# Bringing x into the odd mixer through memory blocks, with merged last down groups and a later exponential of the forget gate

## The chip, the cores and the metric

The kernel runs on one core of one Trainium2 chip. The metric is the device time of one execution in microseconds (us), as the median of the runs shown. The instruction streams are called by their engines: TensorE (PE in the profile), VectorE (DVE), ScalarE (ACT), GpSimd (POOL) and SyncE (SP). SP only issues transfers here, and ACT and POOL issue some of theirs.

## The reference

A block of 256 tokens with 2048 features goes through two layers, all in float32:

```python
def reference(x, ...):
    for i in range(2):
        h = rms_norm(x, norm_mix_g[i])
        if i % 2 == 0:      # even mixer: spatial gating and pooling
            ...
        else:               # odd mixer: attention with a forget gate, 16 heads of 128
            p = h @ w_in_odd[o]
            q, k, v = ...                         # columns 0:2048, 2048:4096, 4096:6144
            f_logit = p[..., 3 * C_WIDTH:] + b_forget[o]      # 16 columns
            log_f = jax.nn.log_sigmoid(f_logit)
            att = forgetting_attention(q, k, v, log_f)
            mix = att @ w_out_odd[o]
        x = x + mix
        x = x + conv_ffn(rms_norm(x, norm_ffn_g[i]), w_up[i], conv_w[i], conv_b[i], w_down[i])
    return rms_norm(x, final_norm_g)
```

`conv_ffn` multiplies with `w_up` (2048 x 11264), convolves over three tokens, gates with a silu and multiplies with `w_down` (5632 x 2048). In `forgetting_attention` the running sum `c` of `log_f` over the tokens is added to the logits of each head: `logits + c[q] - c[k]`, ahead of the softmax.

## The kernel before

**Weights.** All weights stream through the core once, in pieces of 1 MB (128 x 2048 numbers), 368 of them in a fixed order. SP loads piece c into slot c % 4 of `raw`. ACT rounds it to TensorE's single-pass format (`high`, L466, into `w_high`), DVE takes the rest (`low`, L878, into `w_low`), and TensorE multiplies with both. Each activation is split in the same way, into `h_split` or `y_split`, so a product is three passes: high by high, high by low and low by high. ACT and DVE work three pieces ahead of TensorE (`LEAD = 3`): in step c they prepare piece c + 3, which waits until TensorE has used piece c - 1. `load(c + 4)` waits until DVE is done with piece c. The order of the instructions on each engine is written out by hand; semaphores tie the engines together, and `fenced` makes an engine wait for its own instruction.

**The end of layer 0.** The feed-forward part takes `w_up` in 11 groups (`NG`) of features. For each of them a down product of four pieces adds to the 256 x 2048 block `x`: a piece covers 512 features of the group and 512 columns of `x`. The four blocks of 512 columns are called column 0 to column 3 here, and the eight last down pieces D0 to D7: before, D0 to D3 are group 9 on columns 0 to 3, and D4 to D7 group 10 on columns 0 to 3. DVE adds each product to `x` from PSUM (`add_to_x`, L940).

**From x to the mixer.** The odd mixer needs `x` with the features on the partitions. Columns 0, 1 and 2 are turned by TensorE (`transpose_x`, L1511, called from `down` with `transposes=True`, eight 128 x 128 transposes a column into PSUM), column 3 by 16 transposes of DVE in 32 x 32 blocks (`turn_blocks`, L931). Then ACT scales with the norm's gain and rounds (`turned_high`, L505), and DVE takes the rest (`turned_low`, L899); `s_turned` counts the columns that are ready (9 to 12 here). The squares of `x` are summed on ACT (`squares`, L488), and the norm's factor per token is spread over the rows by DVE (`spread_rstd`, L970).

**The first mixer pieces**, called M0 to M11, in this order: M0, M1 = v parts 0, 1; M2, M3 = first halves of the panels q0, k0; M4, M5 = v parts 2, 3; M6, M7 = second halves of q0, k0; M8 to M11 = q1 and k1. v part n needs column n, and a half panel two columns. After M3 TensorE computes the forget gate's sums (`forget_sums`, L1783); ACT copies them (L760), DVE adds up and scales, ACT takes an exponential and a logarithm (L763, L764, each behind a load of its function table), and DVE runs the sum over the tokens (L1323), whose end (`cneg`, L1327) raises `s_cq`. On that wait POOL, which stores the 16 rows to memory (L422), loads them spread over all partitions (L432, L434) and adds the causal mask (L437, `s_bias`), and TensorE's first scores.

**The heads.** From M8 on each head goes: scores on TensorE (`scores`), logits with bias and row maximum on DVE (`head_logits`, L1259), exponentials on ACT, one reciprocal on DVE, scaling on ACT, 16 small transposes on DVE (`head_blocks`, L1281), then the product with v on TensorE (`attend`, L1773), a rounding on ACT and the rest on DVE (`head_low`, L1287). Here `attend` waits for both `head_blocks` and the `head_low` of the head before. These steps stand between the weight pieces on each engine:

```python
if k == 10:
    head_blocks(hh, r)
...
if h is not None:
    head_logits(h, psA[:, 2, :], r)      # first group: h = 0 in step 9, h = 1 in step 11
...
low(c + k + LEAD, r)
```

Of the kernel before, what the change touches and what calls it, by code (L numbers as in the profile page):

```python
# [29 lines left out]
P = 128  # L30
RING = 4
LEAD = 3
# [17 lines left out]
def build(nc, x_in, norm_mix_g, norm_ffn_g, final_norm_g, w_in_even, ln_v_g, ln_v_b, w_spatial,  # L50
          b_spatial, w_pool, pool_scale, w_out_even, w_in_odd, b_forget, w_out_odd, w_up, conv_w,
          conv_b, w_down, out, c_dram):
# [21 lines left out]
    N_END = N_FFN[1] + 12 * NG  # L74
    OUT0_ORDER = [(c, q) for c in range(4) for q in (2, 3, 0, 1)]
# [8 lines left out]
    A_OUT0, A_FFN, A_OUT1 = 0, [4, 4 + 4 * NG + 4], 4 + 4 * NG  # L84
# [6 lines left out]
    X_READY = [0, A_OUT0, A_FFN[0] + 4 * (NG - 1), A_OUT1, A_FFN[1] + 4 * (NG - 1)]  # L91
# [8 lines left out]
    OUT = out[0].rearrange("(t p) d -> p t d", p=P)  # L100

    with ExitStack() as ctx:
# [67 lines left out]
        xT = [work[:, c0:c0 + 1024].rearrange("p (k t) -> p k t", k=4) for c0 in (0, 1024, 2048, 4096)]  # L170
        scaled = raw[:, 0:2, :]
# [34 lines left out]
        s_turn = sem("x_turned")  # L206
        s_turn_hi = sem("turned_high")
# [75 lines left out]
        def turned_bank(s, n, kk):  # L283


            if s == 0 and n == 0:
                return psT[:, min(kk, 2), TOK * (kk // 3):TOK * (kk // 3) + TOK]
            if s in (1, 3) or (s, n) in ((0, 3), (2, 3)):
                return xT[n if s else 0][:, kk, :]
            return psT[:, 2 * (n % 2) + kk // 2, TOK * (kk % 2):TOK * (kk % 2) + TOK]  # L290
# [9 lines left out]
        def _(sp):  # L300
# [47 lines left out]
            def load_ffn(l):  # L348
# [24 lines left out]
                down(B + 124, NG - 2)  # L373
                down(B + 128, NG - 1)
# [71 lines left out]
        def _(a):  # L446
# [47 lines left out]
            def turned_high(s, n):  # L494
# [3 lines left out]
                for kk in range(4):  # L498
# [150 lines left out]
            def ffn(l):  # L649
# [40 lines left out]
                for k in range(16):  # L690
                    if k >= 14 and l == 0:
                        turned_high(s + 1, k - 14)
# [30 lines left out]
                    if l == 0 and k >= 13:  # L723
                        squares(s + 1, k - 13)
# [131 lines left out]
        def _(ve):  # L856
# [64 lines left out]
            def turn_blocks(s, n, tokens):  # L921
# [10 lines left out]
                if 3 in tokens:  # L932
                    ins.then_inc(s_turn, 1)

# [233 lines left out]
            def ffn(l):  # L1168
# [48 lines left out]
                for k in range(16):  # L1217
                    if k >= 14 and l == 0:
                        turned_low(s + 1, k - 14)
                    low(c + k + LEAD)  # L1220
                    if k == 0:
# [18 lines left out]
                    if k >= 8 and not (l == 1 and k >= 12):  # L1240
# [50 lines left out]
            def heads_of_group(first, r=0):  # L1291
                c, hh = N_MIX1 + 12 * first, 4 * first
                for k in range(12):
                    if first == 0 and k == 0:
                        turned_low(2, 2)
                        turn_blocks(2, 3, (0, 1))
                        mean_square(2)
                        turn_blocks(2, 3, (2, 3))
                    if first == 0 and k == 1:
                        rstd_columns(2)  # L1300
                    if first == 0 and k == 2:
                        turned_low(2, 3)
# [9 lines left out]
                    if first == 0 and k == 5:  # L1312
# [8 lines left out]
                        link(ve.tensor_scalar(fl, fl, 0.0, None, ALU.min))  # L1321
                        ve.wait_ge(s_fe, 1)
# [5 lines left out]
                    low(c + k + LEAD, r)  # L1328
                    if h is not None:
                        head_inverse(h, r)  # L1330
                    if first == 0 and k == 2:
                        spread_rstd()
                        link(ve.tensor_scalar(q_rstdT, rstdT[:, :], float(P) ** -0.5, None, ALU.mult))
# [531 lines left out]
```

## Time and profile before

| | |
|---|---|
| median of 3 runs | 2085.55 us (2085.26 to 2085.55) |
| profiled execution | 2085.45 us, span of its instructions 2083.8 us |
| granted TensorE clock, mean | 0.999 |
| busy: TensorE, DVE, ACT, POOL | 2075.3, 1595.5, 1053.6, 26.0 us |
| moved | 397.17 MB, mean 191 GB/s |

The span runs from the first to the last instruction; 1.65 us of the execution's time lie around it. TensorE's ends are modelled, so its groups in a timeline overlap the next one's start by a few tenths; the distance between two starts is the safer measure.

### The profile page before, as it was taken

Reading aid. Unit: us, or ns where it says so; the run is one execution under the profiler, and the core shown is the slowest. Engines: PE = TensorE matmul, PEld = TensorE weight load, DVE = VectorE, ACT = ScalarE, POOL = GpSimd, SP = SyncE. Lnnn points to the kernel's source line nnn. Section 1 sums busy time; section 2 is a strip of 40 time slices with the busy share of each in tenths; the row PEclk is TensorE's granted clock in tenths of the full one; section 3 lists DMA queues with packets and bytes.
Section 4 is the critical chain, followed back from the end, with each engine's and each line's share of the span. In section 5 each row is a group of like instructions: output and inputs, shape, how many; then the busy total and the mean of one; then the engine's idle time right before and its main releaser. Section 6 shows DMA issues by size and latency. Waiting matters only on the chain.

```text
span 2083.8 us, 29774 instructions
## 1 busy us (share of the span) xinstructions
PE 2075.3 (100%) x10936; PEld 1793.1 (86%) x10936; DVE 1595.5 (77%) x2058; ACT 1053.6 (51%) x1103; POOL 26.0 (1%) x56
## 2 busy tenths in 40 slices
PE   9999999999999999999999999999999999999998
PEld 8888888888888888888888888888888888888887
DVE  7988886777667776778788788997776677767676
ACT  7554564445444544456544454465454445444454
POOL 0000000000000000000100000000000000000000
PEclk9999999999999999999999999999999999999999
DMA  8656565655565655655565565556555556556553
GB/s 281 221 164 220 179 206 181 201 195 184 184 198 183 203 181 181 201 187 169 185 214 157 189 209 183 169 187 216 193 185 187 195 183 205 182 181 200 182 191 113
DMA packets 317636, 397.17 MB, mean 191 GB/s; under 512 B 8676, under 2 KB 241420, under 8 KB 317452
## 3 DMA queue, kind: packets, MB, share of 16 engines
q1 hardware_dynamic: 313948, 391.40, 56.7%
q0 software_dynamic: 1056, 3.16, 0.7%
q10 hardware_dynamic: 2576, 1.85, 0.3%
q8 instruction: 36, 0.59, 0.1%
q14 instruction: 20, 0.16, 0.0%
HBM read 394.28 MB, written 2.11 MB: 190 GB/s over the span
## 4 chain that ended last, share of the span: by engine, by line
PE 100%; DVE 0%; issue 0%; ACT 0%; DVEq 0%; ACTq 0%
PE ps_turned L1443 38%; PE ps_straight L1482 35%; PE ps_turned L1452 20%; PE ps_straight L1443 1%; PE ps_turned L1482 1%; PE ps_straight L1452 1%; PE ps_straight L1530 1%; PE ps_straight L1763 0%; PE ps_straight L1773 0%; PE ps_turned L1511 0%; PE ps_straight L1518 0%; PE ps_straight L1638 0%; PE ps_straight L1783 0%; PE ps_straight L1710 0%; PE ps_straight L1707 0%; PE ps_straight L1706 0%
## 5 line engine op out<-in xcount | busy, mean ns | idle before, releaser
L878 DVE TENSOR_TENSOR w_low<-w_raw,w_high 128x2048 fp32r<-128x2048 f32 x368 | 842.3, 2292 | 327.2 <-ACT w_high L466 296.9
L466 ACT ACTIVATE w_high<-w_raw 128x2048 fp32r<-128x2048 f32 x367 | 702.6, 1918 | 659.2 <-PE ps_straight L1482 280.6
L1443 PE MATMUL ps_turned<-h_split,w_high 128*128 128x512 f32 x3456 | 802.9, 390 | 0.0
L1443 PEld LDWEIGHTS ps_turned<-h_split,w_high 128*128 128x128 f32 x3456 | 643.7, 188 | 130.4
L1452 PEld LDWEIGHTS ps_turned<-h_split,w_low 128*128 128x128 f32 x3456 | 425.4, 192 | 6.2 <-DVE w_low L878 0.2
L1452 PE MATMUL ps_turned<-h_split,w_low 128*128 128x256 f32 x3456 | 429.2, 283 | 0.0
L1482 PE MATMUL ps_straight<-w_high,y_split 128*128 128x512 f32 x1792 | 425.5, 390 | 0.1
L1482 PEld LDWEIGHTS ps_straight<-w_high,y_split 128*128 128x128 f32 x1792 | 336.0, 188 | 70.0 <-issue 0.5
L1482 PE MATMUL ps_straight<-w_low,y_split 128*128 128x512 f32 x896 | 221.3, 389 | 0.0
L1482 PEld LDWEIGHTS ps_straight<-w_low,y_split 128*128 128x128 f32 x896 | 168.2, 188 | 34.9
L1149 DVE SCALAR_TENSOR_TENSOR work<-work,conv_columns 128x256 f32<-128x256 f32 x352 | 154.6, 481 | 11.0
L940 DVE TENSOR_TENSOR x<-x,ps_straight 128x512 f32<-128x512 f32 x182 | 116.8, 683 | 54.3 <-PE ps_straight L1482 53.5
L632 ACT ACTIVATE work<-work,conv_columns 128x256 f32<-128x256 f32 x176 | 95.6, 591 | 60.1 <-DVE work L888 60.0
L475 ACT ACTIVATE work<-ps_turned 128x512 f32<-128x512 f32 x108 | 64.7, 599 | 79.7 <-PE ps_turned L1443 66.0
L884 DVE TENSOR_TENSOR work<-ps_turned,work 128x512 f32<-128x512 f32 x108 | 74.5, 690 | 27.6 <-ACT work L475 24.8
L1482 PE MATMUL ps_straight<-w_high,h_split 128*128 128x512 f32 x352 | 85.6, 395 | 0.0
L1281 DVE STREAM_TRANSPOSE work<-work 32x96 f32<-32x96 f32 x256 | 69.1, 270 | 13.1 <-DVE small L1269 7.9
L1482 PEld LDWEIGHTS ps_straight<-w_high,h_split 128*128 128x128 f32 x352 | 65.5, 188 | 13.3
L888 DVE TENSOR_TENSOR work<-work,rstd_rows 128x512 f32<-128x512 f32 x103 | 71.3, 692 | 3.5
L931 DVE STREAM_TRANSPOSE work<-x 32x256 f32<-32x256 f32 x160 | 69.8, 436 | 2.4
L1482 PE MATMUL ps_straight<-w_low,h_split 128*128 128x512 f32 x176 | 43.6, 389 | 0.0
L1482 PEld LDWEIGHTS ps_straight<-w_low,h_split 128*128 128x128 f32 x176 | 33.0, 188 | 6.9
(210 smaller groups left out, 777.7 us busy)
## 6 DMA issues: line engine op xcount, KB each, us to landing
w_raw<-in_w_up SPq DMA_DIRECT2D x176, 1024.0 KB, 5.0
w_raw<-in_w_down SPq DMA_DIRECT2D x88, 1024.0 KB, 5.0
w_raw<-in_w_in_odd SPq DMA_DIRECT2D x48, 1024.0 KB, 5.4
w_raw<-in_w_in_even SPq DMA_DIRECT2D x22, 1024.0 KB, 5.7
w_raw<-in_w_out_even SPq DMA_DIRECT2D x16, 1024.0 KB, 5.0
w_raw<-in_w_out_odd SPq DMA_DIRECT2D x16, 1024.0 KB, 5.1
w_raw<-in_w_in_even SPq DMA_DIRECT2D x4, 512.0 KB, 5.9
work<-c_rows POOLq DMA_DIRECT2D x8, 256.0 KB, 6.4
```

The source lines that it names most:

```text
L466: a.activation(wh[:, s, :], raw[:, s, :], ACT.Copy).then_inc(s_high, 1)
L632: ins = a.activation(cc[j % 2][:, m, :], up[:, m, 2:], ACT.Identity, scale=taps[:, l, 2, bass.ds(i, 1)], bias=taps[:, l, 3, bass.ds(i, 1)])
L878: ve.tensor_tensor(wl[:, s, :], raw[:, s, :], wh[:, s, :].bitcast(F32), ALU.subtract).then_inc(s_low, 1)
L884: fenced(ve.tensor_tensor(to, src, spare, ALU.add), s_added, at(q + 1, 4, r))
L888: return ve.tensor_tensor(ap, ap, factor.unsqueeze(1).to_broadcast([P, 2, TOK]), ALU.mult)
L931: ins = ve.transpose(dst, src)
L940: ins = ve.tensor_tensor(xc, xc, psA[:, 2 * (i % 2) + t, :] if sums is None else sums[:, t, :], ALU.add)
L1149: ins = ve.scalar_tensor_tensor(out=c[:, m, :], in0=up[:, m, 2 - back:TOK + 2 - back], scalar=taps[:, l, 2 - back, bass.ds(i, 1)], in1=c[: ...
L1281: ins = ve.transpose(dst, src)
L1443: ins = pe.matmul(ps[:, 2 * slot + m, :], hi[:, kk, P * m:P * m + P], acts[:, K, :], start=(K == 0 and not narrow_ran), stop=(K == KC - 1) ...
L1452: ins = pe.matmul(ps[:, 2 * slot + m, TOK:], lo[:, kk, P * m:P * m + P], acts[:, K, 0:TOK], start=(K == 0 and opens), stop=(K == KC - 1), ...
L1482: return pe.matmul(ps[:, 2 * slot + t, :], acts[:, k0 + kk, a0:a0 + P], weights[:, kk, :], start=begin, stop=end)
```

## The change

The down pieces of the last two groups of layer 0 are taken in another order (`LAST0`, as (second group, column)): both groups of a column add up in PSUM, and `add_to_x` runs once per column: column 0 after D3, column 1 after D4, column 2 after D5, column 3 after D7. As soon as a column is summed, ACT issues four stores of it to a buffer in device memory (`x_dram`, 128 KB each). When they have landed, SP issues four loads that bring it back with the 32 x 32 blocks already in their turned places, in runs of 32 numbers (128 bytes; `X_BLOCKS`). One transpose of DVE then turns all blocks of the column (128 x 1024). TensorE's transposes of `x` for the odd mixer and DVE's 16 block transposes of column 3 go away. The loads stand in SP's queue between those of the mixer pieces, two columns behind the load of M3, one behind M4's, one behind M5's. The forget gate's sums move from ahead of M4 to ahead of M5, ACT's copies of them from step 5 to step 6, and the exponential and logarithm from ahead of step 5's rounding to the end of step 6, behind the rounding of M9 and `copy_low_half`. DVE's scan moves likewise.

```diff
+    LAST0 = [(0, 0), (0, 1), (0, 2), (1, 0), (1, 1), (1, 2), (0, 3), (1, 3)]
+    X_COLUMNS = x_dram.rearrange("n a t i c -> n i a t c")
+    X_BLOCKS = x_dram.rearrange("n a t i (k j b) -> n j a (t i k) b", k=4, j=4)
...
+        blocks = [work[:, c0:c0 + 1024] for c0 in (0, 1024)]
@@ SP
+            def fetch_blocks(n):
+                sp.wait_ge(s_column[n], 64)
+                if n >= 2:
+                    sp.wait_ge(s_turn, 4 * 2 + n - 1)
+                for j in range(4):
+                    sp.dma_start(blocks[n % 2][32 * j:32 * j + 32, :].rearrange("p (m b) -> p m b", b=32),
+                                 X_BLOCKS[n, j]).then_inc(s_blocks[n % 2], 16)
             for n, (j, k) in enumerate(MIX1_FIRST):
                 load(N_MIX1 + n, quad(W_IN1, k, 8) if j == "v" else half(W_IN1, k, 256 * (j // 2) + D * (j % 2)))
+                if n == 3:
+                    fetch_blocks(0)
+                    fetch_blocks(1)
+                if n in (4, 5):
+                    fetch_blocks(n - 2)
@@ ACT
+            def store_column(n):
+                a.wait_ge(s_xadd, X_READY[2] + n + 1)
+                for i in range(4):
+                    a.dma_start(X_COLUMNS[n, i], x[32 * i:32 * i + 32, :, 512 * n:512 * n + 512])\
+                        .then_inc(s_column[n], 16)
...
-                    if k >= 14 and l == 0:
-                        turned_high(s + 1, k - 14)
+                    if k == 15 and l == 0:
+                        turned_high(2, 0)
                     high(c + k + LEAD)
-                    if l == 0 and k >= 13:
-                        squares(s + 1, k - 13)
+                    if l == 0 and 12 <= k < 15:
+                        store_column(k - 12)
+                        squares(2, k - 12)
@@ ACT, heads_of_group
                     if first == 0 and k == 0:
-                        turned_high(2, 2)
+                        turned_high(2, 1)
+                        store_column(3)
                         squares(2, 3)
                     if first == 0 and k == 2:
+                        turned_high(2, 2)
+                    if first == 0 and k == 3:
                         turned_high(2, 3)
-                    if first == 0 and k == 5:
+                    if first == 0 and k == 6:
                         a.wait_ge(s_f, 1)
                         a.activation(f_xl, psA[0:HEADS, 2, TOK:], ACT.Copy).then_inc(s_fT, 1)
                         fenced(a.activation(f_wl, psA[2 * HEADS:3 * HEADS, 2, 0:TOK], ACT.Copy), s_fT, 2)
-                        a.wait_ge(s_fl, 1)
-                        link(a.activation(fe, fe, ACT.Exp))
-                        fenced(a.activation(fe, fe, ACT.Ln, bias=1.0), s_fe, 1)
                     high(c + k + LEAD, r)
                     if k in ((5, 7, 9, 11) if first else (6, 7, 9, 11)):
                         copy_low_half(Q_MIX1 + 4 * first + j, j % 2, c + k, r)
+                    if first == 0 and k == 6:
+                        a.wait_ge(s_fl, 1)
+                        link(a.activation(fe, fe, ACT.Exp))
+                        fenced(a.activation(fe, fe, ACT.Ln, bias=1.0), s_fe, 1)
@@ DVE
+            def turn_within_blocks(n):
+                ve.wait_ge(s_blocks[n % 2], 64 * (n // 2 + 1))
+                ve.transpose(xT[2 + n % 2].rearrange("p k (g a) -> p k g a", a=32),
+                             blocks[n % 2].rearrange("p (g k b) -> p k g b", g=8, k=4)).then_inc(s_turn, 1)
...
-                    if k >= 14 and l == 0:
-                        turned_low(s + 1, k - 14)
+                    if k == 15 and l == 0:
+                        turn_within_blocks(0)
+                        turned_low(2, 0)
                     low(c + k + LEAD)
+                    if k == 15 and l == 0:
+                        turn_within_blocks(1)
+                        add_to_x(X_READY[2] + 3, 3, c + k)
+                        turned_low(2, 1)
-                    if k >= 8 and not (l == 1 and k >= 12):
+                    if l == 0 and k in (11, 12, 13):
+                        add_to_x(X_READY[2] + k - 11, k - 11, c + k, sums=psT if k == 13 else None)
@@ DVE, heads_of_group: turn_within_blocks(2) and turned_low(2, 2) ahead of low in step 2; turn_within_blocks(3),
@@ turned_low(2, 3) and spread_rstd behind it; the scan behind take_qk(0) in step 6
@@ TensorE
-                    if transposes and n >= 1:
-                        transpose_x(2, n - 1)
+            def last_two_down0(c):
+                pe.wait_ge(s_actlo, 2 * NG - 2)
+                for n, (second, q) in enumerate(LAST0):
+                    ...
+                    straight_quad(c + n, (0, 1, 0, 1)[q], Y, 4 * second, second == 0, second == 1,
+                                  ps=psT if q == 2 else psA)
@@ TensorE, heads_of_group
-                        pe.wait_ge(s_turned, 9 + min(k, 2) if k < 4 else 12)
+                        pe.wait_ge(s_turned, (9, 10, 10, 10, 11, 12)[min(k, 5)])
-                        if k == 4:
+                        if k == 5:
                             forget_sums()
```

## Rows read from the trace of the kernel before

**Rows 1.** The page: shares by engine in the chain that ended last.

```profile
PE 100%; DVE 0%; issue 0%; ACT 0%; DVEq 0%; ACTq 0%
```

**Rows 2.** Waits of TensorE over the whole span: in total, times, longest.

```profile
PE ps_straight L1518 <- DVE ones L862: 1.2, 1, 1.2
```

**Rows 3.** Timeline of TensorE, D5 to M0: start, length, engine, line, tiles, count.

```profile
951.77 3.79 PE L1482 MATMUL ps_straight<-w_high,y_split 128*128 128x512 f32 x16
...
957.21 1.03 PE L1511 MATMUL ps_turned<-ident,x 128*128 128x128 f32 x8
...
970.68 3.89 PE L1482 MATMUL ps_straight<-w_high,h_split 128*128 128x512 f32 x16
```

**Rows 4.** Timeline of DVE, 915 to 1030: as before, idle time ahead in brackets.

```profile
957.41 1.28 DVE L940 TENSOR_TENSOR x<-x,ps_straight 128x512 f32<-128x512 f32 x2 [1.09 <-PE ps_straight L1482]
...
962.09 2.29 DVE L878 TENSOR_TENSOR w_low<-w_raw,w_high 128x2048 fp32r<-128x2048 f32 x1 [1.13 <-issue]
...
965.63 1.68 DVE L899 SCALAR_TENSOR_TENSOR h_split<-ps_turned,feature_columns,h_split 128x256 fp32r<-128x256 f32 x4
...
990.61 3.98 DVE L970 STREAM_TRANSPOSE rstd_rows<-small 32x64 f32<-32x64 f32 x16
...
1005.11 0.68 DVE L1323 TENSOR_TENSOR_SCAN work<-work 16x256 f32<-16x256 f32 x1 [3.30 <-ACT work L764]
...
1006.82 0.28 DVE L1327 TENSOR_SCALAR work<-work 16x256 f32<-16x256 f32 x1
...
1024.88 0.74 DVE L1259 SCALAR_TENSOR_TENSOR work<-ps_straight,small,work 128x128 f32<-128x128 f32 x2 [1.21 <-PE ps_straight L1763]
```

**Rows 5.** DMA, whole span: SP's queue, then issues with KB and us to landing.

```profile
q1 hardware_dynamic: 313948, 391.40, 56.7%
...
w_raw<-in_w_down SPq DMA_DIRECT2D x88, 1024.0 KB, 5.0
...
result<-w_raw SPq DMA_DIRECT2D x3, 128.0 KB, 1.9
```

**Rows 6.** DMA in 890 to 900 us: the queue of ACT's own transfers.

```profile
q10 hardware_dynamic: 2096, 0.13, 14.1%
```

**Rows 7.** A stretch: length, busy times by engine, clock, DMA share, GB/s.

```profile
12.00:16.00 4.00, 4.00 (x21) 3.32 (x20) 2.78 (x2) 0.89 (x1) 0.00 (x0) 1.00 1.05 389
```

**Rows 8.** Timeline of ACT, 885 to 1030.

```profile
958.34 1.71 ACT L505 ACTIVATE h_split<-ps_turned,feature_columns 128x256 fp32r<-128x256 f32 x4 [3.03 <-PE ps_turned L1511]
960.09 1.92 ACT L466 ACTIVATE w_high<-w_raw 128x2048 fp32r<-128x2048 f32 x1
...
1001.57 1.28 ACT L763 ACT_TABLE_LOAD   x1 [4.14 <-DVE work L1319]
...
1004.59 0.42 ACT L764 ACTIVATE work<-work 16x256 f32<-16x256 f32 x1
...
1013.12 0.60 ACT L475 ACTIVATE work<-ps_turned 128x512 f32<-128x512 f32 x1 [3.59 <-PE ps_turned L1443]
```

**Rows 9.** Groups of DVE by shape: busy, mean ns of one.

```profile
L931 DVE STREAM_TRANSPOSE work<-x 32x256 f32<-32x256 f32 x160 | 69.8, 436 | 2.4
L1281 DVE STREAM_TRANSPOSE work<-work 32x96 f32<-32x96 f32 x256 | 69.1, 270 | 13.1 <-DVE small L1269 7.9 <-DVE work L888 1.9
```

**Rows 10.** Timeline of POOL, 1000 to 1060: the bias of heads 0, 1, then 2, 3.

```profile
1007.76 0.66 POOL L422 DMA_DIRECT2D c_rows<-work  x1 [1005.07 <-DVE work L1327]
...
1017.17 2.17 POOL L437 TENSOR_TENSOR work<-work,causal 128x256 f32<-128x256 f32 x2 [5.80 <-DMA work<-c_rows]
...
1047.64 1.43 POOL L437 TENSOR_TENSOR work<-work,causal 128x256 f32<-128x256 f32 x2 [5.35 <-DMA work<-c_rows]
```

**Rows 11.** Timeline of DVE, 1059 to 1130: the rest of head 2.

```profile
1076.89 0.42 DVE L1287 TENSOR_TENSOR y_split<-ps_straight,y_split 128x256 f32 x1 [0.18 <-DVE work L1281]
```

**Rows 12.** Timeline of TensorE, 1022 to 1110: products with v of heads 0 and 3.

```profile
1042.01 0.59 PE L1773 MATMUL ps_straight<-work 128*128 128x256 f32 x2
...
1078.32 0.59 PE L1773 MATMUL ps_straight<-work 128*128 128x256 f32 x2
```

More of the change, by code:

```diff
@@ L51, in build @@
           b_spatial, w_pool, pool_scale, w_out_even, w_in_odd, b_forget, w_out_odd, w_up, conv_w,
-          conv_b, w_down, out, c_dram):
+          conv_b, w_down, out, c_dram, x_dram):
     D = x_in.shape[2]
@@ L206, in build @@
         s_turn = sem("x_turned")
+        s_column = [sem(f"x_column_stored{i}") for i in range(4)]
+        s_blocks = [sem(f"x_blocks_landed{i}") for i in range(2)]
         s_turn_hi = sem("turned_high")
@@ L372, in load_ffn @@
                 panels(B + 120, NG - 1, 1)
-                down(B + 124, NG - 2)
-                down(B + 128, NG - 1)
+                if l == 0:
+                    for n, (second, q) in enumerate(LAST0):
+                        row = 4 * (NG - 2 + second)
+                        load(B + 124 + n, W_DOWN[l][:, row:row + 4, 512 * q:512 * q + 512])
+                else:
+                    down(B + 124, NG - 2)
+                    down(B + 128, NG - 1)
             load_ffn(0)
@@ L1321, in heads_of_group @@
                         link(ve.tensor_scalar(fl, fl, 0.0, None, ALU.min))
+                    low(c + k + LEAD, r)
+                    if h is not None:
+                        head_inverse(h, r)
+                    if first == 0 and k == 2:
+                        turn_within_blocks(3)
+                        turned_low(2, 3)
+                        spread_rstd()
+                        link(ve.tensor_scalar(q_rstdT, rstdT[:, :], float(P) ** -0.5, None, ALU.mult))
+                    if k in ((5, 7, 9, 11) if first else (6, 7, 9, 11)):
+                        take_qk((k - 5) // 2, first, r)
+                    if first == 0 and k == 6:
                         ve.wait_ge(s_fe, 1)
@@ L1327, in heads_of_group @@
                         fenced(ve.tensor_scalar(cneg, sums[0:HEADS, :], -1.0, None, ALU.mult), s_cq, 1)
[L1328 to L1333, printed above, removed]
-                    if k in ((5, 7, 9, 11) if first else (6, 7, 9, 11)):
-                        take_qk((k - 5) // 2, first, r)
             heads_of_group(0)
@@ L1679, in panel, with down @@
                 turned_panel(c, j, H, r)
-            def down(l, g, c, r=0, frm=0, transposes=False):
-                if frm:
-                    pe.wait_ge(s_actlo, 22 * l + 2 * g + 2)
-                else:
-                    pe.wait_ge(s_actlo, at(22 * l + 2 * g + 2, 2, r))
+            def down(l, g, c, r=0):
+                pe.wait_ge(s_actlo, at(22 * l + 2 * g + 2, 2, r))
                 for n in range(4):
@@ L1689, in down @@
                     pe.wait_ge(s_xadd, at(i - 1, 4, r))
[L1690 to L1692 removed]
+                    straight_quad(c + n, n % 2, Y, 0, True, True, r)
+            def last_two_down0(c):
+                pe.wait_ge(s_actlo, 2 * NG - 2)
+                for n, (second, q) in enumerate(LAST0):
+                    if n == 0:
+                        pe.wait_ge(s_xadd, X_READY[2] - 1)
+                    if n == 1:
+                        pe.wait_ge(s_xadd, X_READY[2])
+                    if n == 2:
+                        pe.wait_ge(s_added, Q_FFN[0] + 4 * NG - 1)
+                    if n == 3:
+                        pe.wait_ge(s_actlo, 2 * NG)
+                    if n == 6:
+                        pe.wait_ge(s_xadd, X_READY[2] + 2)
+                    straight_quad(c + n, (0, 1, 0, 1)[q], Y, 4 * second, second == 0, second == 1,
+                                  ps=psT if q == 2 else psA)
             def last_down(c):
@@ L1742, in ffn @@
                     panel(l, NG - 1, j, B + 116 + 2 * j)
-                down(l, NG - 2, B + 124)
                 if l == 0:
-                    down(l, NG - 1, B + 128, frm=1, transposes=True)
+                    last_two_down0(B + 124)
                 else:
+                    down(l, NG - 2, B + 124)
                     last_down(B + 128)
```

21 lines of the change are left out of this document (11 added, 10 removed).

## The prediction

> **What bounds the kernel now.** I read the chain of waits first: TensorE alone makes up the chain that ended last [rows 1]. The list of waits says the same from the other side: TensorE's longest wait on another engine is 1.2 us, once, at the start [rows 2]. So a step on ACT, DVE, POOL or a queue costs nothing as long as TensorE finds its operand ready, and the change can win only what it takes from TensorE's own instructions. What it can lose is every place where an operand comes later than TensorE wants it. The rest is therefore a comparison of arrival times around the end of layer 0 and the first heads. The sum goes against the profiled execution, 2085.45 us (2083.8 us of span and 1.65 around it), 0.1 us under the median of the runs.
>
> **What TensorE saves.** D5 starts at 951.77 and the first transposes at 957.21, so a straight piece takes 5.44 us [rows 3]. From 951.77 to M0 at 970.68 stand three pieces and three sets of transposes: 18.91 us, against 3 x 5.44 = 16.32 without the transposes. The saving is 2.59 us, and M0 could start at 957.21 + 2 x 5.44 = 968.09, M1 at 973.53. The new order of the down pieces has the same eight pieces, so it costs TensorE nothing. The four additions to x that go are DVE's, 1.28 us each [rows 4]; DVE is off the chain, so I count them at nothing.
>
> **Columns through memory.** Column 0 is summed after D3, which ends at 951.77 - 5.44 = 946.3; with the addition of 1.28 us [rows 4] it is there at 947.8, columns 1 and 2 at 953.2 and 958.7. ACT issues four stores; one of 128 KB landed 1.9 us after its issue [rows 5], so with four issues in a row and weights beside them I take 4 us: 952. SP then issues the loads, but behind M3's weights, which go out when DVE is done with D7's low half (950.9) and take 5.0 us [rows 5]: the blocks start at 956. A column is 4096 runs of 128 bytes, 256 on each of 16 engines. No row shows 128-byte runs. The nearest are the forget gate's weights, 2048 runs of 64 bytes: 2096 packets took 14.1% of 10 us x 16 engines, 10.8 ns each [rows 6]. From above I bound them by the mean of SP's packets, 56.7% x 2083.8 x 16 / 313948 = 60 ns [rows 5], though those carry ten times the bytes. I take 12 ns: 3.1 us a column; column 0 lands at 959 to 960. In the upper bound it is 15.4 us.
>
> The Trainium skill has a rule against such runs: "DMA: Bandwidth & Descriptors", Specifications, asks for 512 B at least for line rate and says that shorter runs are read, modified and written. Read as a quarter of the full rate of 389 GB/s [rows 7], that is an estimate of 5.4 us a column instead of 3.1; column 0 would land near 962, and the sum below would change by under 1 us. The 64-byte packets at 10.8 ns [rows 6] stand at 5.9 GB/s an engine, so the loss of rate is real here and its size is open.
>
> DVE comes to the first transpose after the low half of M1: ACT rounds that piece after D5 (957.4 + 1.92 [rows 8]), DVE takes 2.29 us more [rows 4]: 961.8. The blocks have then been there for about 2 us. The transpose of 128 x 1024 has no row; a line through 270 ns at 96 elements and 436 at 256 [rows 9] gives 1.04 ns an element and 1.24 us. The column then needs 1.71 us on ACT, and DVE's 1.68 us that start behind ACT's first half [rows 8, 4]: column 0 is ready at 965.9, 2.2 us before M0. Next on ACT M2's rounding (1.92), on DVE its low half (2.29), the transpose of column 1 (1.24), column 3's addition (1.28), then the split of column 1: 965 + 1.9 + 2.3 + 1.3 + 1.3 + 1.7 with the hand-overs (about 0.1 each) is 973.9. M1 wants it at 973.5, so TensorE waits 0.4 us. Columns 2 and 3 follow in the same way, each behind a rounding and a low half, column 3 also behind its own store and load: I get 988 against M4 at 990.5, and 995.7 against the gate's sums at 996. No wait, with 0.3 us to spare on the second. SP's weights behind the loads lose some 3 to 9 us, and no TensorE piece wants them for more than 10. The DVE step spread_rstd (3.98 us [rows 4]) now stands behind column 3, which makes M6 and M7 later on DVE (1002, 1004.5) but not late (1005, 1010.7). **After M6** TensorE is 2.59 - 0.4 = 2.2 us ahead.
>
> **The forget gate's running sum.** This edit I do not cost at nothing. The exponential now waits for `copy_low_half`, which waits for the end of M6. Before, that copy started at 1013.12 [rows 8]; with TensorE 2.2 us ahead it starts at 1010.9 and ends at 1011.5. The two table loads and two functions take 1004.59 + 0.42 - 1001.57 = 3.44 us [rows 8]: 1015.0. DVE from the scan to the end of `cneg` takes 1007.10 - 1005.11 = 2.0 us [rows 4]: `s_cq` at 1017.1, where it was 1007.1, that is 10.0 us later. Behind it stands POOL: from `cneg` to a bias that is ready it took 1017.17 + 2.17 - 1007.10 = 12.2 us; with the next tile's addition of 1.43 it is 11.5 [rows 10]. I take 11.5, since DVE stands idle beside it now: bias at 1028.6. Before, it was ready at 1019.3, and DVE used it at 1024.88 [rows 4] when the scores came; the cover was 5.5 us, and the delay is 9.3. So the first head's logits come 3.7 us later than before, in absolute time. Behind them in DVE's order wait the low half of M12 and all that follows, TensorE not yet. About 0.7 us comes back, because ACT's next copy no longer waits for TensorE; the chain of heads runs 3.0 us late.
>
> Its cover is short. The rest of head 2 ended at 1076.89 + 0.42 = 1077.3 [rows 11], and TensorE asked for it at 1078.32 [rows 12]: 1.0 us of slack. The heads follow one another on DVE and ACT with hardly any idle time, so a delay is handed down from head to head. By head 3 TensorE is where that chain is, less the slack: 3.0 - 1.0 = 2.0 us later than before. It had been 2.2 ahead, so the waits at the products with v add up to 4.2 us. In the next group DVE waits for TensorE again, and nothing more is lost or won back.
>
> **Sum.** 2085.45 - 2.59 + 0.4 + 4.2 = 2087.4 us, 0.1% above before. What a measurement of this kernel can tell from no change is 0.2%, or 4.2 us.
>
> **Rivals.**
> *The saving is kept.* Bias ready by 1025 instead of 1028.6 would leave the heads on time; then the time is 2085.45 - 2.59 plus the 0 to 0.4 us at M1: 2082.9 to 2083.3. For it speaks only that POOL's 11.5 us rest mostly on transfers that were shared with weights; against it that the second tile's transfers took as long. Anything between this and the forecast is a shorter bias wait.
> *Both waits grow.* If the runs cost 25 to 40 ns, column 0 lands at 962 to 966 and what follows shifts: 1 to 4 us at M1, handed on to M6, to the exponential and to the heads in full, and more at column 1 above 30 ns. The time is 2089 to 2095.
> *Slower, by the loads.* At the upper bound of 60 ns a column takes 15.4 us on SP's queue, with the next column and M4's weights behind it. Column 0 lands at 971 (TensorE waits 7 us at M0), column 1 at 986.5 (10 at M1), column 2 after M4's weights at 1004.5 (1 at M4), column 3 at 1022.6 (13 at the gate's sums); with the 4 us of the heads 2085.45 - 2.6 + 31 + 4 = 2118. It decides from about 30 ns a run. The rows speak against it, since 64 bytes cost 10.8 ns [rows 6], but runs that are read from memory only just written have no row. The Trainium skill's "DMA: Bandwidth & Descriptors", Rules for kernel authors, warns more sharply: a plain DMA with a rearranged access pattern took 19 times as long as a hardware transpose. That would be an estimate of 19 x 1.35 = 26 us a column (512 KB at 389 GB/s [rows 7] being 1.35) and beyond 2150; the runs here keep 128 bytes in order, and no run here shows such a price.
> *Faster by more than 4.2 us* has no source, since TensorE has no idle time to give back.
>
> **How the numbers follow.** The forecast (2085 to 2089.6) has 0.63, the saving kept or mostly kept 0.13, both waits grown 0.11, the loads 0.10, something unseen on the fast side 0.03. The predicted time is the first one's, 2087.4. The range 2083.2 to 2091 leaves out the loads, the upper half of the grown waits, the fast end and a little of the kept saving, 0.2 in all. Within 0.2% are the first two, 0.76; slower 0.21; faster 0.03.
>
> **What would show it.** In the profile after: no transposes between D5 and M0, and 5.44 us between starts; the loads of a column landing 3 to 4 us after M3's weights; a first wait of TensorE at M1 under 1 us; the scan near 1015 instead of 1005; POOL's first addition near 1027; DVE idle ahead of the first logits (L1259 in the numbering before) for some 5 us; and waits of TensorE of 1 to 2 us at the products with v of heads 0 to 3. The prediction is wrong if the first column lands after 962, if those products do not wait, or if TensorE waits at M4 or at the gate's sums.

## The result and the profile after

The changed kernel took 2089.14 us in the median of 20 runs (2088.10 to 2090.75), the kernel before 2085.43 (2084.95 to 2085.60): a ratio of 1.0018, with an interval of 1.0012 to 1.0024. That is 3.7 us more, 1.7 above the forecast and inside its range. The interval does not reach 1, so a change of this size, 0.18%, can be told from none, although the prediction put that limit at 0.2%. The profiled execution took 2089.85 us, with a span of 2088.1.

TensorE's waits on other engines in the changed kernel, over the whole span (in total, times, longest), answer to [rows 2]. Line 1827 is the first matmul of `scores`, 1838 that of the product with v, 927 the scaling of a panel (`take_qk`), 1333 `head_blocks`:

```profile
PE ps_straight L1827 <- DVE work L927: 2.9, 1, 2.9
PE ps_straight L1571 <- DVE ones L901: 1.2, 1, 1.2
PE ps_straight L1838 <- DVE work L1333: 0.6, 1, 0.6
PE ps_straight L1583 <- DVE w_high L954: 0.3, 1, 0.3
```

Two are new. The timeline of TensorE shows the stretch of [rows 3], from D6 to M1:

```profile
956.71 3.79 PE L1535 MATMUL ps_straight<-w_high,y_split 128*128 128x512 f32 x16
...
962.14 3.79 PE L1535 MATMUL ps_straight<-w_high,y_split 128*128 128x512 f32 x16
...
967.59 3.79 PE L1535 MATMUL ps_straight<-w_high,h_split 128*128 128x512 f32 x16
...
973.23 3.92 PE L1535 MATMUL ps_straight<-w_high,h_split 128*128 128x512 f32 x16
```

The steps are 5.43 and 5.45 us, and M1 starts 5.64 after M0: a wait of 0.2 us. The gate's sums start at 995.53, 5.63 after M4: again some 0.2 us of wait. TensorE then asks for the first scores at 1021.36, where it did so at 1024.03 before: it is 2.7 us ahead, 0.5 of them because D5 already starts that much earlier. So 2.2 of the 2.59 us are still there, and what the change loses beyond that comes behind. Further on in the same timeline, which answers to [rows 12]:

```profile
1021.36 0.38 PE L1827 MATMUL ps_straight<-work 128*128 128x128 f32 x2
...
1040.08 0.70 PE L1838 MATMUL ps_straight<-work 128*128 128x256 f32 x2 [0.58 <-DVE work L1333]
...
1049.35 0.80 PE L1827 MATMUL ps_straight<-work 128*128 128x128 f32 x2 [2.86 <-DVE work L927]
1049.94 1.06 PE L1828 MATMUL ps_straight<-work 128*128 128x256 f32 x2
1050.44 6.40 PE L1535 MATMUL ps_straight<-w_high,h_split 128*128 128x512 f32 x16
...
1058.50 0.59 PE L1838 MATMUL ps_straight<-work 128*128 128x256 f32 x2
...
1082.55 0.59 PE L1838 MATMUL ps_straight<-work 128*128 128x256 f32 x2
```

and in the kernel before the first scores, the scores of head 2 and the product behind them:

```profile
1024.03 0.38 PE L1762 MATMUL ps_straight<-work 128*128 128x128 f32 x2
...
1048.14 0.38 PE L1762 MATMUL ps_straight<-work 128*128 128x128 f32 x2
...
1054.27 0.59 PE L1773 MATMUL ps_straight<-work 128*128 128x256 f32 x2
```

The product of head 3 starts 4.2 us after its place before. TensorE waits 0.6 us at the first product and 2.9 at the scores of head 2, and then M13's 16 matmuls take 6.40 us where M12's took 3.92. From 1049.35 to 1058.50 it needs 9.15 us; before, the same work took 1054.27 - 1048.14 = 6.13. The 3.0 us are no wait. Stretches of the changed kernel (length, busy times of TensorE, weight loads, DVE, ACT, POOL, then the granted clock, DMA share, GB/s) say what they are:

```profile
1044.00:1046.40 2.40, 2.40 (x12) 1.72 (x10) 2.26 (x2) 0.93 (x5) 1.13 (x2) 1.00 0.92 312
1046.40:1049.30 2.90, 0.09 (x1) 0.00 (x0) 1.38 (x2) 2.38 (x5) 0.00 (x0) 0.90 0.99 247
1049.30:1050.40 1.10, 1.05 (x4) 0.96 (x5) 0.77 (x3) 1.10 (x1) 0.00 (x0) 0.50 0.84 261
1050.40:1052.00 1.60, 1.60 (x5) 1.31 (x4) 1.52 (x7) 1.60 (x2) 1.26 (x2) 0.50 1.00 356
1052.00:1054.00 2.00, 2.00 (x6) 1.53 (x5) 1.91 (x8) 0.36 (x1) 0.16 (x1) 0.50 0.16 57
1054.00:1056.00 2.00, 2.00 (x7) 1.52 (x7) 1.58 (x3) 0.00 (x0) 0.00 (x0) 0.62 0.00 0
1056.00:1058.00 2.00, 2.00 (x10) 1.68 (x9) 1.97 (x4) 0.00 (x0) 0.00 (x0) 1.00 0.00 0
```

The granted clock falls to 0.50, the lower of its two levels (1.2 of 2.4 GHz), in the wait, and is back at 1.00 after some 6 us of work at half speed: 1.10, 1.60, 2.00 and, by the mean of 0.62, 0.76 of the next 2.00, together 6.2 us. Half speed loses half of that, 3.1 us, which accounts for the 3.0.

Why the scores wait is read from DVE's timeline of the changed kernel, which answers to [rows 4]:

```profile
1014.61 0.68 DVE L1384 TENSOR_TENSOR_SCAN work<-work 16x256 f32<-16x256 f32 x1 [1.99 <-ACT work L824]
...
1016.32 0.28 DVE L1388 TENSOR_SCALAR work<-work 16x256 f32<-16x256 f32 x1
...
1028.43 0.74 DVE L1311 SCALAR_TENSOR_TENSOR work<-ps_straight,small,work 128x128 f32<-128x128 f32 x2 [5.84 <-POOL work L464]
...
1047.88 0.69 DVE L923 TENSOR_TENSOR work<-ps_turned,work 128x512 f32<-128x512 f32 x1 [1.63 <-ACT work L502]
1048.61 0.69 DVE L927 TENSOR_TENSOR work<-work,rstd_rows 128x512 f32<-128x512 f32 x1
```

and POOL's, which answers to [rows 10]:

```profile
1017.27 0.66 POOL L449 DMA_DIRECT2D c_rows<-work  x1 [1014.58 <-DVE work L1388]
...
1026.90 1.43 POOL L464 TENSOR_TENSOR work<-work,causal 128x256 f32<-128x256 f32 x2 [6.04 <-DMA work<-c_rows]
```

The running sum is ready at 1016.6 instead of 1007.1, the bias 11.7 us behind it, at 1028.3, and DVE stands idle for 5.84 us ahead of the first logits. Behind them in its order stand the logits of head 1 and then panel k1 (`take_qk(3)`), ready at 1049.3: that is what the scores of head 2 wait for. In the kernel before the panel's last step was

```profile
1045.76 0.69 DVE L888 TENSOR_TENSOR work<-work,rstd_rows 128x512 f32<-128x512 f32 x1
```

so it was ready at 1046.45, 1.7 us ahead of the scores at 1048.14. Now it comes 2.9 us later and TensorE 1.7 earlier, at 1046.5; less the 1.7 of slack, that is the wait.

### The profile page after: what moved, and what is told of

The parts are those of the page before. It is cut to its first block, busy times and chain, and to the rows that moved or that the text cites. A ratio compares the mean times of both kernels' runs of the same rounds, so it can differ in the third digit from the quotient of the medians.

```text
span 2088.1 us, 29692 instructions
## 1 busy us (share of the span) xinstructions
PE 2076.0 (99%) x10912; PEld 1792.0 (86%) x10912; DVE 1588.0 (76%) x2038; ACT 1053.6 (50%) x1103; POOL 25.2 (1%) x56
## 4 chain that ended last, share of the span: by engine, by line
PE 92%; DVE 5%; issue 1%; ACT 1%; POOL 0%; DMA 0%; DVEq 0%; ACTq 0%; POOLq 0%
PE ps_turned L1496 35%; PE ps_straight L1535 32%; PE ps_turned L1505 19%; DVE w_low L917 2%; DVE work L970 1%; PE ps_turned L1535 1%; PE ps_straight L1496 1%; PE ps_straight L1583 1%; DVE work L1194 0%; PE ps_straight L1505 0%; DVE x L985 0%; DVE h_split L938 0%; PE ps_straight L1828 0%; DVE work L927 0%; DVE work L923 0%
## 5 line engine op out<-in xcount | busy, mean ns | idle before, releaser
L1535 PE MATMUL ps_straight<-w_high,y_split 128*128 128x512 f32 x1760 | 417.7, 390 | 0.1
L1535 PEld LDWEIGHTS ps_straight<-w_high,y_split 128*128 128x128 f32 x1760 | 330.1, 188 | 68.9 <-issue 0.6
L985 DVE TENSOR_TENSOR x<-x,ps_straight 128x512 f32<-128x512 f32 x172 | 110.3, 682 | 52.5 <-PE ps_straight L1535 51.8
L970 DVE STREAM_TRANSPOSE work<-x 32x256 f32<-32x256 f32 x144 | 62.8, 436 | 2.2
L532 ACT ACTIVATE h_split<-work,feature_columns 128x256 fp32r<-128x256 f32 x52 | 23.7, 504 | 41.5 <-DVE work L970 29.6
```

Source lines behind the costliest of these rows:

```text
L970: ins = ve.transpose(dst, src)
L985: ins = ve.tensor_tensor(xc, xc, psA[:, 2 * (i % 2) + t, :] if sums is None else sums[:, t, :], ALU.add)
L1535: return pe.matmul(ps[:, 2 * slot + t, :], acts[:, k0 + kk, a0:a0 + P], weights[:, kk, :], start=begin, stop=end)
```

## The experiments

Theory A: the late exponential makes the bias late, with it DVE's chain of the first heads, and TensorE waits for that chain and then runs at the low clock. Theory B: the columns' way through memory costs the time. Times are medians of 10 or 11 runs, beside the kernel before in the same set (2085.4 to 2085.6). The changed kernel took 2089.14 in its first set and 2089.20 in a later one.

**One part undone.** On ACT and likewise on DVE, against the changed kernel:

```diff
@@ ACT, step 6, behind the copies of the gate's sums
+                        a.wait_ge(s_fl, 1)
+                        link(a.activation(fe, fe, ACT.Exp))
+                        fenced(a.activation(fe, fe, ACT.Ln, bias=1.0), s_fe, 1)
@@ DVE: the scan from the end of step 6 to step 5, ahead of low
```

> The changed kernel with only the order of the forget gate undone: exponential and logarithm stand on ACT right behind the copies of the gate's sums again, ahead of the rounding of M9, and DVE's scan stands ahead of the low half of M8. Theory A (the late running sum costs the time: bias late, DVE's heads late, TensorE waits at the second head pair's scores and then runs at the low clock): the scan ends near 1012 instead of 1016.6, the bias is ready near 1023 instead of 1028.3, TensorE waits neither at the first product with v (0.6 us in the changed kernel) nor at the scores of head 2 (2.9), and the clock stays at 1.0. DVE is now held by the scan and may bring the addition of panel q0 1 to 1.5 us late for M8. Time 2083.0 to 2084.6. Rival B (the columns' way through memory costs the time, in bandwidth or in late weights): no change against the changed kernel, 2088 to 2090.

Measured: 2085.39 us, ratio 0.9999 (0.9990 to 1.0008); 3.7 less than the changed kernel, 0.8 above the expected range. No wait at the products or the scores, and the clock is 1.0. The bias was ready only at 1026.3, not near 1023, and TensorE still did not wait for what hangs on it. The new wait is at M8. The trace names no releaser for it; in the kernel M8 waits for DVE's addition of panel q0, which ended at 1018.31. A second wait of 0.5 us stands at the gate's sums. TensorE's timeline of this run, M8:

```profile
1018.40 3.91 PE L1494 MATMUL ps_turned<-h_split,w_high 128*128 128x512 f32 x16 [1.50 <-issue]
```

So the later exponential bought something too: the early one holds DVE 3.7 us at the scan, with the panel behind it. The two waits give back most of what the transposes saved.

**One part alone.** The kernel before, with only the exponential, the logarithm and the scan moved as the change moves them.

> The kernel before with only the exponential, the logarithm and the scan put behind the rounding and the copy of step 6, as the change does; the columns still go through TensorE. Theory A: the scan waits for the end of M6 as in the changed kernel, which here is 2.6 us later; sum ready near 1019.3, bias near 1031, the first logits 6 us later than before; TensorE waits about 0.7 us at the first product with v and 3 us at the scores of head 2, and loses 3 us more at the low clock behind that wait: 2091 to 2093. Rival B: the later exponential is hidden, 2085.2 to 2086.

Measured: 2090.86 us, ratio 1.0026 (1.0017 to 1.0036), 0.1 under the expected range. This edit alone costs 5.3 us, and theory B has nothing to work with here, since no column goes through memory. TensorE's waits in this run have the same places as in the changed kernel:

```profile
PE ps_straight L1764 <- DVE work L889: 2.9, 1, 2.9
PE ps_straight L1520 <- DVE ones L863: 1.2, 1, 1.2
PE ps_straight L1775 <- DVE work L1282: 0.4, 1, 0.4
```

and M13 behind them is as slow as there, at a clock of 0.50 from 1052 to 1058:

```profile
1053.07 6.39 PE L1484 MATMUL ps_straight<-w_high,h_split 128*128 128x512 f32 x16
```

**The wait filled.** The changed kernel, in the first group of heads only:

```diff
+                    if fill and k == 0:
+                        pe.wait_ge(s_added, Q_MIX1 + 3)
+                        for _ in range(10):
+                            pe.matmul(psT[:, 0, :], H[:, 0, 0:P], H[:, 0, :], start=True, stop=True)
                     if first and k in (0, 2):
                         scores(hh - 2 + k // 2, SB, first - 1, r)
```

> The changed kernel with ten matmuls that no one reads (128 x 512 into a free PSUM bank, some 2.2 us) in TensorE's wait ahead of the scores of head 2, in the first group of heads alone. Clock theory: the wait lasts as long as before (until DVE is done with panel k1), but TensorE is not idle in it, the granted clock stays at 1.0 and the scores and M13 take 0.5 and 5.7 us again instead of 1.1 and 8.1: 3 us less than the changed kernel, 2085.7 to 2086.5. Rival (M13 is slow for another reason, such as the transfers or DVE beside it): the same as the changed kernel, 2088.5 to 2090.

Measured: profiled 2087.97 us, median 2088.48 (1.0014, 1.0005 to 1.0023). The clock is 1.00 in every stretch from 1040 to 1058, and M13's matmuls take 3.99 us. TensorE's timeline:

```profile
1046.60 2.43 PE L1884 MATMUL ps_turned<-h_split 128*128 128x512 f32 x10
1049.74 0.46 PE L1827 MATMUL ps_straight<-work 128*128 128x128 f32 x2 [0.71 <-DVE work L927]
1050.04 0.60 PE L1828 MATMUL ps_straight<-work 128*128 128x256 f32 x2
1050.28 3.99 PE L1535 MATMUL ps_straight<-w_high,h_split 128*128 128x512 f32 x16
...
1080.55 0.67 PE L1838 MATMUL ps_straight<-work 128*128 128x256 f32 x2 [0.41 <-issue]
```

The profile confirms the mechanism: what made M13 slow is the clock behind an idle TensorE. The gain is smaller than expected: the median is 2.0 us above the clock theory's range and at the lower end of the rival's. The product of head 3 comes 2.2 us after its place before, and it waits there: with the clock held, TensorE runs into DVE's chain again (the trace names no releaser; the rest of head 2 on DVE ended 0.1 us ahead of it). The median fell by only 0.7 us, and that against another set, so I ran the changed kernel again beside one with 16 filling matmuls.

> The changed kernel with 16 unread matmuls (3.5 us) instead of 10 ahead of the scores of head 2, so that TensorE is not idle there in any repetition; where the wait is the 2.9 us of the trace they make it 0.6 us longer. Clock theory: M13 and the scores run at full speed (3.0 us less), 0.6 us are given back, so 2.4 us less than the changed kernel in the same set: 2086.5 to 2087.2. If the low clock plays a smaller part in the repeated runs than in the profiled one, as the medians of the run with ten matmuls suggested (0.7 us less instead of 1.9), it is 2088 to 2089.5.

> The changed kernel once more, unaltered, beside the run above on the same chip: 2088.8 to 2089.5, with waits at the first product with v and at the scores of head 2 as in its first profile.

Measured: 2088.24 (2087.75 to 2088.62) against 2089.20 (2088.29 to 2090.21): 0.96 less, where the clock theory had 2.4, and in the range for a low clock that plays a smaller part. Nine of the 11 runs of the changed kernel lie above all 11 with the wait filled. In the profile of the filled run the clock is 1.00 from 1040 to 1058 and M13 takes 4.00 us. In this second profile of the changed kernel the wait is again 2.9 us, but the slow stretch is shorter:

```profile
1049.30:1050.40 1.10, 0.22 (x2) 0.23 (x3) 0.79 (x2) 0.93 (x1) 0.00 (x0) 1.00 0.65 118
1050.40:1052.00 1.60, 1.60 (x6) 1.30 (x6) 1.51 (x6) 1.60 (x2) 0.54 (x1) 0.58 0.99 341
1052.00:1054.00 2.00, 2.00 (x6) 1.58 (x5) 1.91 (x8) 1.19 (x1) 0.88 (x2) 0.50 0.65 226
1054.00:1056.00 2.00, 2.00 (x10) 1.58 (x10) 1.54 (x6) 0.00 (x0) 0.00 (x0) 0.98 0.00 0
```

From the scores of head 2 to the next product it takes 1058.05 - 1050.18 = 7.87 us, 1.7 more than 6.13, where the first profile had 3.0 more. The clock fell only when the scores were already running, and by the rows above 3.4 us of work were at half speed instead of 6.2. With the 0.6 us that 16 matmuls add, 1.1 us of difference were to be expected from this profile, and 0.96 were measured. So the low clock is real in the repeated runs too. It cost 3.0 us in one profile and 1.7 in the other, and the medians speak for about 1.6; why one execution has more of it than another stays open.

**The gate's work fitted in.** Against the changed kernel: DVE's sums of the gate one step earlier (ahead of the low half of M7), the exponential directly behind ACT's copies, the scan ahead of the low half of M9, and the transpose of column 1 ahead of the low half of M2.

> The changed kernel with the gate's work fitted in: DVE's sums of the gate go ahead of the low half of M7 (one step earlier), the exponential and logarithm directly behind the copies, the scan ahead of the low half of M9; and the transpose of column 1 goes ahead of the low half of M2. Theory A: sum ready near 1011, bias near 1022.5, logits when the scores come; panel q0 in time for M8; no wait at M1. Only the saving of the transposes is left: 2085.43 - 2.6 = 2082.8 (2082.5 to 2083.5). Rival B: 2088 or more. A third view, that the exponential must stand early at the cost of a wait at M8, would leave this one no better than the run with the exponential early.

Measured: the profiled execution took 2084.29 us, but the median is 2086.44, from 2084.29 to 2087.26 (1.0004, 0.9995 to 1.0013). That is 2.9 us above the expected range, and no better than the run with the exponential early, as the third view had it. The sum is ready at 1010.8, as expected, but the bias only at 1025.0: POOL's store, loads and addition took 14.2 us from `cneg`, not 11.5. The sum is 5.8 us earlier than in the changed kernel and the bias only 3.3. M1 still starts 5.74 us after M0. The scores of head 2 still wait:

```profile
1045.99 0.49 PE L1826 MATMUL ps_straight<-work 128*128 128x128 f32 x2 [0.42 <-DVE work L926]
```

A profile shows one execution. Whether the slower ones came from a later bias or later columns was the next question.

**The copy in between.** Against the fitted run, in the first group of heads only:

```diff
                     if k in (9, 11):
                         head_exp(hh + (k - 9) // 2, r)
-                        head_scale(hh + (k - 9) // 2, r)
+                        if first:
+                            head_scale(hh + (k - 9) // 2, r)
                     if k in ((5, 7, 9, 11) if first else (6, 7, 9, 11)):
                         copy_low_half(Q_MIX1 + 4 * first + j, j % 2, c + k, r)
+                    if first == 0 and k in (9, 11):
+                        head_scale(hh + (k - 9) // 2, r)
```

> The run with the gate's work fitted in, and in the first group of heads ACT's copy for the panels q1 and k1 goes between a head's exponentials and its scaling, so that ACT makes the copy while it waits for DVE's reciprocal and DVE no longer waits 1.6 us per head for it. Theory A: the chain of the first two heads gets 1.6 us shorter each, the 0.4 us wait at the scores of head 2 that the fitted run still shows goes away with a margin of some 2 us for a bias that lands later: 2082.5 to 2083.3, and the repeated runs lie within 0.6 us of each other instead of 3. Rival: the spread of the fitted run comes from the columns' loads and not from the heads; then the median stays near 2086.4 and the spread at 3 us.

Measured: 2083.75 us, 2083.05 to 2084.24. That is 0.5 us above the expected range, with twice the expected spread, and 1.6 us under the kernel before. The ratio 0.9992 has an interval of 0.9983 to 1.0001: faster is likely, since all 11 runs lie under the lowest of the kernel before in this set (2084.84), but the interval does not exclude no change. The spread fell from 3.0 to 1.2 us with an edit that touches the heads alone, so it had reached the time through the heads, and the third view falls. In this profile the bias was ready even later than in the fitted run, at 1026.8, and TensorE's list of waits holds no line but the one at the start:

```profile
PE ps_straight L1573 <- DVE ones L903: 1.2, 1, 1.2
```

**The same edit on the changed kernel**, with its late exponential.

> The changed kernel with its late exponential, and only ACT's copies of the first group of heads put between the exponentials and the scaling. Theory A says that what counts is when DVE's chain of heads reaches panel k1 and the products with v, not when the gate's sum is ready: the sum stays at 1016.6, the bias at 1028.3, but panel k1 is ready near 1046 instead of 1049.3, TensorE waits less than 1 us ahead of the scores of head 2, the clock stays at 1.0: 2083.2 to 2084.8. If the late sum itself were the cost (POOL's transfers, the bias), it stays at 2088 to 2089.5.

Measured: 2085.00 us (0.9997, 0.9988 to 1.0006), 0.2 above the expected range and 4.1 us less than the changed kernel, with the sum as late as there (1016.5) and the bias at 1028.0. Panel k1 is ready at 1045.8 instead of 1049.3. TensorE waits 0.3 us at the scores of head 2 and 0.4 at the product of head 3. What costs time is how late DVE's chain comes to panel k1, not the sum as such. Two copies on ACT moved by one place are worth about as much as the exponential's place (4.1 and 3.7 us, too close to rank).

**The transposes back.** Against the run with the copy in between:

```diff
                     straight_quad(c + n, (0, 1, 0, 1)[q], Y, 4 * second, second == 0, second == 1,
                                   ps=psT if q == 2 else psA)
+                    if n >= 5:
+                        for i in range(8):
+                            pe.transpose(psT[:, 2 + i // 4, P * (i % 4):P * (i % 4) + P], ident[:, :], ident[:, :])
```

> The fitted run with the copy in between, and TensorE does 24 transposes of 128 x 128 that no one reads, eight behind each of D5, D6 and D7, where the kernel before had them. If the whole saving of the change is TensorE's own time in them, this costs 2.6 us: 2085.1 to 2085.9, the time of the kernel before. If the saving came from the order of the down pieces or from ACT's and DVE's shorter work, less than 1 us.

Measured: 2085.79 us in the median, 2.0 more than without; the spans of the two profiles differ by 2084.1 - 2081.5 = 2.6. So the saving of the change is TensorE's own time in the transposes: the new order of the pieces and the shorter work of ACT and DVE leave, by the medians, at most 0.6 us of it.

**The columns twice.** Against the run with the copy in between: each load followed by a copy of the same runs from memory to memory (`x_again`), and DVE waits for both.

```diff
+                    sp.dma_start(x_again[n, j], X_BLOCKS[n, j]).then_inc(s_blocks[n % 2], 16)
@@ DVE
-                ve.wait_ge(s_blocks[n % 2], 64 * (n // 2 + 1))
+                ve.wait_ge(s_blocks[n % 2], 128 * (n // 2 + 1))
```

> The run before with each of the 16 column loads followed by a second copy of the same 128-byte runs, from device memory to device memory, and DVE waiting for both; it doubles the runs of a column to 8192. By the price in the changed kernel's trace (13.2 ns a packet) a column takes 6.8 us instead of 3.4, and SP's eight issues 5.8 us instead of 2.9: column 0 is whole at 963 to 965 instead of about 960, where DVE comes at 961.6. TensorE then waits 0 to 1 us at M0, 2 to 4 at M1 and up to 2 at the gate's sums, as the rival in which both waits grow had it: 2085 to 2089. If the runs were hidden with much room, no change: 2083. If writing to memory makes the copies much slower than 13 ns, above 2092.

Measured: 2088.93 us (1.0017, 1.0008 to 1.0027), 5.2 more than without. DVE got column 0 at 965.8, and M0 and M1 wait. TensorE's timeline:

```profile
969.93 5.53 PE L1538 MATMUL ps_straight<-w_high,h_split 128*128 128x512 f32 x16 [2.10 <-DVE h_split L941]
...
978.93 3.93 PE L1538 MATMUL ps_straight<-w_high,h_split 128*128 128x512 f32 x16 [1.65 <-DVE h_split L941]
```

Behind the wait at M0 its matmuls take 5.53 us instead of 3.79, at a clock of 0.59 and 0.56 in the two stretches from 970 to 974. The waits (3.8 us) and this loss (1.7) make up the cost within 0.3. Columns 2 and 3, and the gate's sums, were in time. The path of the first two columns is hidden with little room: twice the packets, half of which also write to memory, cost twice what the change saves.

## Why the prediction came out as it did

**What TensorE saves: right.** 2.59 us forecast; 2.6 between the spans of the profiles with and without transposes, 2.0 between the medians.

**Columns through memory: right in the price and in the waits, too short in the time of a column.** A packet of 128 bytes was bounded by 10.8 and 60 ns and taken at 12. In the changed kernel's trace from 957 to 963 us SP's queue (q1) carried column blocks almost alone, and beside it ACT's queue (q10) carried the stores:

```profile
q10 hardware_dynamic: 580, 0.94, 52.8%
q1 hardware_dynamic: 3408, 0.43, 46.8%
```

That is 0.468 x 6 us x 16 / 3408 = 13.2 ns a packet, and 3.4 us a column if the engines had nothing else to do. They had: ACT's stores of the next columns took half of them. From 955 to 961 us SP's queue moved 4261 packets, little more than the 4096 of a column, so column 0 took not quite 6 us instead of 3.1. The sum had priced the stores by their landing alone, not by what they take from the loads. Column 0 still came by 961, against 959 to 960 forecast, and DVE, which came at 961.6, found it there:

```profile
961.61 1.24 DVE L977 STREAM_TRANSPOSE work<-work 128x1024 f32<-128x1024 f32 x1
```

This transpose took 1.24 us, as the line through the two shorter ones had it. M1 waited 0.2 us (0.4 forecast), M4 not. The gate's sums, for which 0.3 us to spare were forecast, had none: some 0.2 us of wait here, 0.3 in the second profile of the changed kernel and 0.5 in the run with the exponential early. At 9.7 GB/s an engine the runs have under half the 20.8 of SP's mean packet (1247 bytes in 60 ns [rows 5]). The Trainium skill's "DMA: Bandwidth & Descriptors", Specifications, wants 512 B for line rate; the trace agrees that 128 bytes lose some. The estimate that I drew from it, a quarter of the rate and 5.4 us a column, was too high by 2 us as a price, and the measurement decides; that column 0 took about that long comes from the stores beside it.

**The forget gate's running sum: right.** Ready at 1016.6 (1017.1 forecast), bias at 1028.3 (1028.6), first logits 3.55 us later than before (3.7). That this edit is what makes the change slower the runs with one part alone and one part undone show: alone it costs 5.3 us, and without it the time is that of the kernel before.

**The heads: the delay right, the place and the size of its cost wrong.** The step that failed is "the waits at the products with v add up to 4.2 us". Of the products of heads 0 to 3 only the first waited, 0.6 us, so by its own sign ("if those products do not wait") the prediction was wrong here. The large wait, 2.9 us, came ahead of the scores of head 2, because panel k1 stands behind the logits of head 1 in DVE's order; I had followed DVE's order only along the heads, and not the panel that lies in it. It comes out of the same delay. The chain itself ran as forecast: in the changed kernel the rest of head 2 ended on DVE at 1079.72 + 0.42 = 1080.1, 2.8 us later than before (3.0 forecast). With the wait filled and the clock held, TensorE reached the product of head 3 there, 2.2 us later than before with ten matmuls and 2.0 with 16, for which 2.0 were forecast. The term that was missing is TensorE's clock, which fell around a wait of 2.9 us and cost 3.0 us in one profile and 1.7 in another.

That the time lies in the range is partly luck: the waits of the heads were 3.5 us and not 4.2, and the clock's cost, which has no term in the sum, happened to fit into the room that the range left. Nor is the clock the whole difference: with the wait filled the medians were 2088.48 and 2088.24, still 1.1 and 0.8 above the forecast (0.6 of the second are the 16 matmuls themselves). What the rest is stays open.

**The rivals.** That the saving is kept needed a bias by 1025; it came at 1028.3. The bias was not the only way, though: with ACT's copies moved, most of the saving was kept in the fitted run with a bias at 1026.8. That both waits grow was tried by doubling the packets: column 0 was there at 965.8, and TensorE waited 2.1 us at M0 and 1.7 at M1, where that rival had 1 to 4 at M1 alone. Slow loads at 60 ns fell with the 13.2.

## What to carry to other kernels

When a step moves on an engine, follow every instruction behind it in that engine's order, not only the chain that the step belongs to: here the wait came through a panel that merely stands in line. An operation that waits for another engine's answer (here a scaling for a reciprocal) is the place to put independent work; doing so was worth 4.1 us on the changed kernel, where the transposes are worth 2.6. And a wait of TensorE can be paid twice, as those of 2.1 and 2.9 us were here: its length and the work at the low clock behind it have to be priced together.

## What had not been expected of the hardware

Around the 2.9 us wait the granted clock was 0.50 for some 6 us of work, although but for 0.6 us TensorE had been busy in the 20 us ahead of it; with unread matmuls in the same wait it stayed at 1.00. After the 1.5 us wait at M8 in the run with the early exponential M8's matmuls took their usual time (3.91 us), after 2.1 us at M0 in the run with the columns twice they took 5.53, and after 1.65 us at M1 of that run 3.93.

POOL's store of 16 KB landed in 2.1 us or in 4.5 from its issue (1013.84 to 1015.97 with the early exponential, 1011.44 to 1015.90 in the fitted run). In the first the busy share of the DMA engines was 0.00 to 0.04 meanwhile, in the second 0.82 to 1.06; the kernel before and the changed kernel, with 0.03, took 2.1 us too. So the slow store goes with other traffic, though no run changed the traffic alone.
